# Position bias in a hybrid attention layer: mirrored row stored 128 times in DRAM, loaded straight into place, without eight turning copies

## The reference

```
rel_idx = jnp.clip(qi - kj + LEFT_PAD, -REL_CLIP, REL_CLIP) + REL_CLIP
bias = rel_bias.astype(jnp.float32)[:, rel_idx]
...
scores = jnp.where(valid[None, None, :, None, :], scores + bias[None, :, None], NEG_INF)
p = jax.nn.softmax(scores, axis=-1).astype(v.dtype)
```

## Time and profile before

| | |
|---|---|
| median of 3 runs | 1122.86 us (1122.79 to 1123.09) |
| span of the profiled execution | 1120.9 us |
| PE busy | 1112.3 us, 99% of the span |
| DVE, ACT, POOL busy | 699.1, 459.8, 162.9 us |
| moved by DMA | 153.63 MB |

### The profile page before, as it was taken

The page is one execution under the profiler, slowest core; times in us unless marked ns, Lnnn a source line. Parts: engine busy times, 40 slices in busy tenths (PEclk is TensorE's granted clock), DMA queues, the critical chain, the costliest instruction groups (busy, mean ns, idle before and its releaser), DMA issues.

```text
span 1120.9 us, 16059 instructions
## 1 busy us (share of the span) xinstructions
PE 1112.3 (99%) x5725; PEld 922.8 (82%) x5725; DVE 699.1 (62%) x1167; ACT 459.8 (41%) x870; POOL 162.9 (15%) x259
## 2 busy tenths in 40 slices
PE   9999999999999999999999999999999999999997
PEld 7887887887888888888888888888888888888886
DVE  6314445435345667786878787777777777555584
ACT  5332452543545555663322323222323257444441
POOL 3400011101110112311122112211211120000031
PEclk9999999999999999999999999999999999999999
DMA  7220101110110255342564446444634699777632
GB/s 263 95 76 20 39 20 39 38 39 20 39 38 20 65 198 188 132 131 90 165 215 159 139 132 215 142 127 162 201 117 147 214 315 373 235 228 231 217 116 84
DMA packets 112087, 153.63 MB, mean 137 GB/s; under 512 B 6984, under 2 KB 72536, under 8 KB 112032
## 3 DMA queue, kind: packets, MB, share of 16 engines
q1 hardware_dynamic: 95440, 95.96, 26.8%
q0 software_dynamic: 15424, 52.74, 14.1%
q10 hardware_dynamic: 1168, 4.20, 1.0%
HBM read 112.74 MB, written 40.13 MB: 136 GB/s over the span
## 4 chain that ended last, share of the span: by engine, by line
PE 98%; DMA 1%; DVE 0%; ACT 0%; issue 0%; SPq 0%; POOL 0%; DVEq 0%; POOLq 0%
PE psum L1171 34%; PE psum L801 24%; PE psum L1198 18%; PE psum L1056 8%; PE psum L976 4%; PE psum L844 3%; PE psum L815 2%; PE psum L825 2%; PE psum L790 1%; PE psum L952 1%; DMA arena<-in_x 1%; PE psum L852 0%; PE psum L945 0%; PE psum L958 0%; PE psum L834 0%; DVE arena L2241 0%
## 5 line engine op out<-in xcount | busy, mean ns | idle before, releaser
L801 PE MATMUL psum<-hT,ws 128*128 128x512 f32 (+1 forms) x1104 | 253.9, 385 | 0.0
L801 PEld LDWEIGHTS psum<-hT,ws 128*128 128x128 f32 x1104 | 197.3, 188 | 39.0 <-issue 0.7
L1171 PE MATMUL psum<-arena_r,ws 128*128 128x512 f32 x960 | 224.1, 389 | 0.0
L1171 PEld LDWEIGHTS psum<-arena_r,ws 128*128 128x128 f32 x960 | 180.2, 188 | 37.4
L1171 PE MATMUL psum<-hT,ws 128*128 128x512 f32 x720 | 169.9, 389 | 0.0
L1171 PEld LDWEIGHTS psum<-hT,ws 128*128 128x128 f32 x720 | 135.1, 188 | 28.0
L1198 PE MATMUL psum<-hT 128*128 128x512 f32 (+1 forms) x600 | 135.2, 385 | 0.0
L1198 PEld LDWEIGHTS psum<-hT 128*128 128x128 f32 x600 | 111.3, 188 | 22.5
L2050 DVE TENSOR_TENSOR misc<-misc,psum 128x512 f32<-128x512 f32 x100 | 68.6, 686 | 48.7 <-PE psum L1171 46.1
L1544 ACT ACTIVATE ws<-o_raw 128x512 fp32r<-128x512 f32 x40 | 25.2, 630 | 138.5 <-DVE o_raw L2028 138.0
L1056 PE MATMUL psum<-ws,hT 128*128 128x512 f32 x348 | 81.7, 392 | 0.0
(11 more groups left out here) (222 smaller groups left out, 1361.5 us busy)
## 6 DMA issues: line engine op xcount, KB each, us to landing
raw<-in_w_ffn_in SPq DMA_DIRECT2D x44, 512.0 KB, 4.0
act_scratch<-arena POOLq DMA_DIRECT2D x77, 256.0 KB, 3.2
raw<-in_w_in SPq DMA_DIRECT2D x22, 512.0 KB, 3.8
arena<-in_w_ffn_out POOLq DMA_DIRECT2D x22, 512.0 KB, 5.5
arena<-act_scratch SPq DMA_DIRECT2D x38, 256.0 KB, 3.5
arena<-in_x SPq DMA_DIRECT2D x16, 512.0 KB, 6.3
raw<-in_w_out SPq DMA_DIRECT2D x16, 512.0 KB, 3.6
raw<-act_scratch SPq DMA_DIRECT2D x26, 256.0 KB, 3.6
```

What stands on the lines that cost most here:

```text
L801: last = mm(PP[pair][:, at:end] if to is None else to, w[wp], hT[:, hp, k, at:end], start=(k == 0 and (wp, hp) == (0, 0)), stop=(k == KT - ...
L1171: last = mm(blocks(bank), w[:, k * P:(k + 1) * P], b_operand(i, part, k), start=fresh_bank and k == 0 and w is hi and part == 0, stop=k == ...
```

## The change

The row is built mirrored, so that a window that starts at 127 - p reads forwards; `ext_d` gets a dimension of 128 copies, and the store writes all of them (source: the 8 partitions of `ext`, each read 128 times). Each partition's load then reads from its own copy, into `bias` itself. The eight turning copies are gone, four on POOL and four on ACT, and with them `bias_turned` and ACT's wait for the loads. Both loads are issued one after the other, and the factors of tiles 5 to 7 come after both. Before the loads POOL waits for `g_spread` (`bias` overlays the rows that the gain is spread from) in place of `v_split`.

```diff
-    ext_d = nc.dram_tensor("bias_scratch", [HEADS, ERW], F32, kind="Internal").ap()
+    ext_d = nc.dram_tensor("bias_scratch", [HEADS, P, ERW], F32, kind="Internal").ap()
...
-            near = P - 1 + CLIP
-            nc.gpsimd.tensor_copy(ext[:, near:ERW], relb[:, REL - 1:REL].broadcast_to([HEADS, ERW - near])
+            far = BAND - CLIP
+            nc.gpsimd.tensor_copy(ext[:, 0:far], relb[:, REL - 1:REL].broadcast_to([HEADS, far])
                                   ).then_inc(ext_ready, 1)
             pool.wait_ge(ext_ready, 1)
-            nc.gpsimd.tensor_copy(ext[:, 0:near], relb[:, CLIP + 1 - P:REL - 1]).then_inc(ext_ready, 1)
+            nc.gpsimd.tensor_copy(ext[:, far:ERW], relb[:, REL - 2:CLIP - P:-1]).then_inc(ext_ready, 1)
             pool.wait_ge(ext_ready, 2)
-            pool.dma_start(ext_d, ext).then_inc(ext_stored, 16)
+            pool.dma_start(ext_d, ext.rearrange("h (o x) -> h o x", o=1).broadcast_to([HEADS, P, ERW])
+                           ).then_inc(ext_stored, 16)
...
             pool.wait_ge(ext_stored, 16)
-            pool.wait_ge(v_split, 4)
+            pool.wait_ge(g_spread, 1)
 
 
             for n in range(2):
-                pool.dma_start(turned, bass.AP(ext_d.tensor, 4 * n * ERW, [[1, P], [ERW, 4], [1, BAND]])
+                pool.dma_start(bias[:, 4 * n * BAND:4 * (n + 1) * BAND].rearrange("p (h b) -> p h b", b=BAND),
+                               bass.AP(ext_d.tensor, 4 * n * P * ERW + P - 1, [[ERW - 1, P], [P * ERW, 4], [1, BAND]])
                                ).then_inc(bias_landed, 16)
-                if n == 0:
-                    for i in range(5, NT):
-                        x_factor(i)
-                    pool.wait_ge(bias_landed, 16)
-                    for h in range(4):
-                        nc.gpsimd.tensor_copy(bias[:, h * BAND:(h + 1) * BAND], turned[:, h, ::-1]
-                                              ).then_inc(bias_turned, 1)
-                        pool.wait_ge(bias_turned, h + 1)
-
-            pool.wait_ge(bias_turned, 8)
+            for i in range(5, NT):
+                x_factor(i)
+            pool.wait_ge(bias_landed, 32)
...
-            act.wait_ge(bias_landed, 32)
-            for h in range(4):
-                go(bias[:, (4 + h) * BAND:(5 + h) * BAND], turned[:, h, ::-1], ACT.Copy).then_inc(bias_turned, 1)
```

More of the change, by code:

```diff
@@ L328, in trunk_layer @@
         consts_made = sem("consts_made")
-        bias_turned = sem("bias_turned")
         bias_ready = sem("bias_ready")
```

## The result

| | before | after |
|---|---|---|
| median | 1122.82 us (1122.57 to 1123.09, 4 runs) | 1185.78 us (1185.09 to 1186.32, 4 runs) |
| span of the profiled execution | 1120.9 us | 1183.1 us |

The ratio is 1.0561 (95% interval 1.0546 to 1.0576). The forecast was 1180 with a range of 1145 to 1200: right in its direction, its place and its size, 5.8 us too low. The span grew by 62.2 us.

A forecast was written before the change was run, and what follows sets the result against it. PE was taken to bound the kernel, so any added wait counts in full. 54.7 us of waiting at tile 5's transposes plus 2.7 us of slow restart, 57.4 us on 1122.86, gave 1180 us, range 1145 to 1200.

The forecast's parts named there:

- What bounds the kernel, and that there is nothing to gain: PE, busy 99% of the span, bounds the kernel; the removed copies lie beside idle time, gain priced at nothing.
- The place: PE's transposes of tile 5, behind DVE's scaling, POOL's factor and POOL's wait for the store: 54.7 us of waiting.
- The size of the store, 58.6 us from issue to landing: POOL's store of 3.14 MB takes 57.1 us of data at the small store's 55 GB/s and lands at 86.75.
- The bounds of 44 and 70 us: Range for the store's data time: 43.8 us at 342 ns a row on 8 engines, 70 us at 45 GB/s.
- The cause of that rate, the source: The store's 8 neighbouring source partitions limit it to 55 GB/s, not the number of engines; chance 0.72.
- The steps behind the landing, 3.85 us: From the store's landing to PE's restart: two load issues 1.70, tile 5's factor 0.87, its scaling 1.28 us.
- The restart, 2.7 us: After its long wait at tile 5, PE runs slowly as at the kernel's start, costing 2.7 us, bounds 0 to 4.
- The sum: 54.7 us of PE waiting plus 2.7 us of restart, 57.4 us on the kernel's 1122.86 us: 1180 us.
- The bias loads, the masks and the parameters, priced at nothing: Transfers and masks behind the store finish before they are wanted, the bias with 50 us of cover: no cost.
- The weight loads of SP, taken to shift with PE at no price: SP's weight loads wait for DVE's splits and so move later together with PE: no cost.
- The full rate (1129.6 to 1132.3): Rival: the store runs at the DMA engines' full rate, 9.1 us, giving 1129.6 to 1132.3 us; chance 0.07.
- The engine-limited case: Rival: engines, eight at full speed or 16 at the slow row rate, limit the store: 1138 to 1148 us; chance 0.12.

The follow-up runs named there:

- the factors first: Changed kernel with POOL making the factors of tiles 5 to 7 before it waits for the store: 1139.2 us, ratio 1.0145.
- steps 2 and 8: Changed kernel with the eight source rows on every second partition (0 to 14) or every eighth (0 to 56): 1154.6 us and 1156.4 us.
- the store in pieces: Changed kernel with the factors first, tile 5's even before the store, and the store cut into four DMAs of a quarter of the columns: 1145.5 us.
- the run with the wide loads: Changed kernel with the factors first and two of SP's weight loads reading whole 4 KB rows (wrong weights) instead of 512-byte pieces: 1135.3 us.
- step 4: Changed kernel with the eight source rows on every fourth partition (0, 4, 8, ... 28): 1141.8 us.

## Why the prediction was right, and where its sum was off

- **What bounds the kernel, and that there is nothing to gain**: right. With the small store in place of the large one, or with the large one fast and the factors first, the change is worth 0.0% (ratios 1.0000 and 0.9997).
- **The place**: right. The wait stood at the transposes of tile 5, put down to the scaling and that to POOL's factor, and moving the factors takes it away.
- **The size of the store, 58.6 us from issue to landing**: mis-sized by 5.6; it took 64.2. The step from the small store's rate was sound in kind, 51 GB/s against 55 assumed: the data took 3.142 MB / 51 GB/s = 61.6 us and not 57.1, which is 4.5 of the 5.6. The rest, 64.2 - 61.6 = 2.6 us around the data against 1.45 assumed, is 1.1. The bounds of 44 and 70 us held. The 51 lies between the two readings of the small store in the earlier trace rows, 55 and 45 GB/s; that the one taken came within 8% was in part luck, as no row told which was nearer.
- **The cause of that rate, the source**: only argued then, shown now by steps 2 and 8, which have the same eight engines and twice the rate, by the store in pieces, which has twice the engines and the same rate, and by the store on SP's queue.
- **The steps behind the landing, 3.85 us**: from the landing at 28.13 + 64.2 = 92.3 to 96.47 it took 4.1. The 0.3 more lie between the landing and POOL's next issue at 92.60, a step that the sum had left out.
- **The restart, 2.7 us**: mis-sized; 0.91 us at the eight transposes and 0.81 at the matmuls, 1.7 us in all. It was read from the kernel's first microseconds, where the transposes stay slow from 1.5 to 7.8 us; here the slow stretch goes from 96.5 to 99.8. The granted clock of 0.50, which the rows of before did not have, now shows the cause for the restart: from 38 us to 99.8 us PE was granted 1.2 GHz in place of 2.4. For the slow transposes at the start of the kernel it is not shown, as the clock reads 1.00 there.
- **The sum**: 60.5 + 1.7 = 62.2 us against 54.7 + 2.7 = 57.4. The span grew by 62.2. The two errors work against each other, 5.8 us too little of waiting and 1.0 too much of restart. The kernel's median is 5.8 above the forecast and not 4.8 because the profiled execution, from which the span is taken, is 0.7 us faster than the median of its kernel, and by rounding.
- **The bias loads, the masks and the parameters, priced at nothing**: right here; the bias was complete at 103.4 and wanted at 156.1, a cover of 53 us. The cover came from PE's own delay. With the factors first most of it was gone, and in the run with the wide loads the parameters did cost 0.7 us and the bias was ready only 0.3 us before it was read.
- **The weight loads of SP, taken to shift with PE at no price**: right here. With the factors first they do not shift, as PE is not late, and they cost 14.6 us; that a slow store holds up other queues' loads is in no term of the sum.
- **The rivals**: the full rate (1129.6 to 1132.3) would have needed all partitions; the run with them gave 1133.4. The engine-limited case (eight engines at full speed, 1140) is what step 4 gave, 1141.8. Both prices were good, for kernels that this one is not.

## What to carry to other kernels

Before a DMA is made larger, look at who stands behind the wait for it, and at how many SBUF ports its partitions reach: a broadcast store out of a few neighbouring partitions is limited by these partitions, 51 GB/s here for eight of them, and putting the same rows four partitions apart gave 3.8 times the rate with no other change to the store. A small transfer in the trace before, read for its GB/s and its busy share together, gave the rate of the large one to 8% here. A slow transfer that nobody waits for is still not free: it holds the DMA engines that others need.

## What the runs showed of the hardware that was not expected

- A store that is limited by its source keeps its DMA engines from other queues almost entirely. Beside it, 512 KB in pieces of 512 bytes took 36.5 us to land (57.9 to 94.4) instead of some 4 us, though eight of sixteen engines were free and took their half at once. From 74 us on the busy engines took one packet of the load for each packet of the store (49 and 49 in 6 us), so that 4 KB pieces got through at some 30 GB/s and 512-byte pieces at 5.
- Twice the engines on the same source partitions moved no more: 51 GB/s with a share of 0.97 as with 0.49.
- Two small loads of 2 KB issued on the same queue behind the store landed with it, 62 us after their issue. With the store on SP's queue, the same two on POOL's took 13.3 and 17.0 us, against 2.5 in the kernel before.
